# First modulation columns of a transformer block: whole rows, six of eight on VectorE and two on TensorE

## The reference, cut to what matters

```
mods = (silu(c) @ w_ada + b_ada).reshape(B, 9, 1024)     # c: 1024, w_ada: 1024 x 9216
n = rmsnorm(x, g_pre[0]) * (1 + scale(0)) + shift(0)     # shift(0), scale(0): first 2048 columns
f = (silu(n @ w_gate) * (n @ w_up)) @ w_down             # 1024 -> 2816 -> 1024
h = x + 0.5 * gate(0) * rmsnorm(f, g_post[0])
```

## Time and profile before

| | |
|---|---|
| median of three executions | 1119.7 us (1119.01 to 1119.9) |
| the profiled execution: time, span | 1119.9 us, 1118.2 us |
| TensorE products busy | 1077.9 us (96%) |
| TensorE weight loads busy | 939.3 us (84%) |
| VectorE busy | 853.0 us (76%) |
| ScalarE busy | 549.4 us (49%) |
| DMA | 266.65 MB, mean 238 GB/s |
| chain that ended last | TensorE 84%, VectorE 6%, DMA 3%, ScalarE 3% |
| mean granted clock of TensorE | 0.989 |

### The profile page before, as it was taken

One profiled execution on the slowest core, in us unless ns is written; L12 is line 12 of the kernel. 1 busy time (PEld: TensorE's weight loads), 2 busy tenths in 40 slices (PEclk: granted clock), 3 DMA queues, 4 the chain that ended last, 5 costly groups with the idle time before them and its releaser, 6 DMA issues.

```text
span 1118.2 us, 16397 instructions
## 1 busy us (share of the span) xinstructions
PE 1077.9 (96%) x6258; PEld 939.3 (84%) x6258; DVE 853.0 (76%) x914; ACT 549.4 (49%) x666; POOL 48.1 (4%) x78
## 2 busy tenths in 40 slices
PE   5799999999999999999999999999999999999996
PEld 3699999979988798888878888888888878888886
DVE  6888888668977787887868988877775787666664
ACT  4434434464675744444464454446454456444442
POOL 0000000011031100000010000001100000000001
PEclk9799999999999999999999999999999999999999
DMA  8899997636433589887569999744553546666641
GB/s 304 312 388 400 398 385 281 208 100 230 152 114 120 181 306 327 310 303 251 195 239 344 342 362 336 250 141 165 187 182 107 162 139 213 222 220 229 207 169 57
DMA packets 147045, 266.65 MB, mean 238 GB/s; under 512 B 9673, under 2 KB 104246, under 8 KB 141750
## 3 DMA queue, kind: packets, MB, share of 16 engines
q1 hardware_dynamic: 145104, 262.69, 67.4%
q0 software_dynamic: 1056, 3.17, 0.8%
q10 hardware_dynamic: 838, 0.15, 0.1%
HBM read 263.34 MB, written 2.65 MB: 238 GB/s over the span
## 4 chain that ended last, share of the span: by engine, by line
PE 84%; DVE 6%; DMA 3%; ACT 3%; issue 2%; POOL 1%; SPq 1%; POOLq 0%; ACTq 0%; DVEq 0%
PE ps L1861 16%; PE ps L1796 12%; PE ps L1798 11%; PE ps L1797 11%; PE ps L1863 8%; PE ps L1842 7%; PE ps L1845 7%; PE ps L1844 7%; DMA w_raw<-in_w_ffn_up 2%; DVE arena L1377 1%; DMA arena<-in_w_ada 1%; DVE w_lo L1150 1%; ACT w_hi L785 1%; ACT nT_both L785 1%; ACT nT L811 1%
## 5 line engine op out<-in xcount | busy, mean ns | idle before, releaser
L1150 DVE TENSOR_TENSOR w_lo<-w_raw,w_hi 128x2048 fp32r<-128x2048 f32 (+3 forms) x170 | 383.1, 2258 | 113.3 <-ACT w_hi L785 112.1
L785 ACT ACTIVATE w_hi<-w_raw 128x2048 fp32r<-128x2048 f32 (+3 forms) x170 | 320.0, 1886 | 272.4 <-PE ps L1798 115.5
L1861 PE MATMUL ps<-nT_both,w_hi 128*128 128x512 f32 x768 | 272.0, 398 | 0.0
L1863 PE MATMUL ps<-nT_both,w_lo 128*128 128x256 f32 x768 | 215.6, 281 | 0.0
L1842 PE MATMUL ps<-nT_both,w_hi 128*128 128x256 f32 x672 | 191.4, 285 | 0.3 <-DVE h_act L1261 0.2
L1845 PE MATMUL ps<-nT_both,w_lo 128*128 128x256 f32 x672 | 190.1, 283 | 0.0
L1844 PE MATMUL ps<-nT_both,w_hi 128*128 128x256 f32 x672 | 190.1, 283 | 0.0
L1861 PEld LDWEIGHTS ps<-nT_both,w_hi 128*128 128x128 f32 x768 | 144.3, 188 | 35.7
L1863 PEld LDWEIGHTS ps<-nT_both,w_lo 128*128 128x128 f32 x768 | 145.0, 189 | 0.9
L1842 PEld LDWEIGHTS ps<-nT_both,w_hi 128*128 128x128 f32 x672 | 128.8, 192 | 2.0 <-DVE h_act L1261 1.2
L1229 DVE SCALAR_TENSOR_TENSOR arena<-arena,c_act 128x3072 f32<-128x3072 f32 (+2 forms) x49 | 129.4, 2650 | 1.3 <-DMA arena<-in_ada_w 0.7
(11 more groups left out here) (278 smaller groups left out, 1203.8 us busy)
## 6 DMA issues: line engine op xcount, KB each, us to landing
arena<-in_w_ada SPq DMA_DIRECT2D x16, 1536.0 KB, 10.5
arena<-in_ada_w SPq DMA_DIRECT2D x16, 1536.0 KB, 8.7
w_raw<-in_w_in SPq DMA_DIRECT2D x46, 512.0 KB, 4.6
w_raw<-in_w_ffn_down SPq DMA_DIRECT2D x44, 512.0 KB, 4.5
w_raw<-in_ffn_w_down SPq DMA_DIRECT2D x44, 512.0 KB, 4.2
w_raw<-in_w_ffn_gate SPq DMA_DIRECT2D x42, 512.0 KB, 6.8
w_raw<-in_w_ffn_up SPq DMA_DIRECT2D x42, 512.0 KB, 8.7
w_raw<-in_ffn_w_gate SPq DMA_DIRECT2D x42, 512.0 KB, 4.1
```

What stands on the lines that cost most here:

```text
L785: copy = lambda o, i: act.activation(o, i, ACT.Copy)
L1150: dve.tensor_tensor(lo(s, n), raw(s, n), hi(s, n).bitcast(F32), ALU.subtract).then_inc(lo_ready[s], 1)
L1861: pe.matmul(ps[:, i, :], hi(s)[:, cols], nT_both[:, kk].rearrange("p a n -> p (a n)"), start=(kk == 0), stop=False, skip_group_check=True)
L1863: last = pe.matmul(ps[:, i, 0:S], lo(s)[:, cols], nT_hi[:, kk, :], start=False, stop=(kk == KD - 1), skip_group_check=True)
```

## The change

The eight pieces of four rows by 512 columns become sixteen rows: for each half eight rows j, each with the 512 columns of shift and the 512 of scale together (`[P, 2, 512]`, 512 KB, in the same runs of 2 KB). Rows 0 to 5 (`ON_DVE`) are summed by VectorE as one vector of 1024 columns (`first_rows`), with one fold of 1024 columns and one fold product for each half. Rows 6 and 7 (`ON_PE`) are not summed by VectorE: `first_rows_sum` on TensorE takes 128 columns of the row as weights and `c_act[:, 0, j]` as one moving column, 8 products for a row, 16 for a half, into a bank of their own. `first_folded` adds the bias to the folded part (four operations), `first_out` adds TensorE's part (one operation) and makes the scale columns. SyncE loads the first weights ahead of rows 6 and 7; it waits for VectorE's sums before it loads over a row, and for TensorE's sum before rows 6 and 7 of half 1; the fourth weights go out after rows 0 and 1 of half 1 are summed. On VectorE the low part of the first weights moves ahead of the last step of half 0's columns. On TensorE the fold products move a little, and `first_rows_sum` stands right before the first products (half 0), and behind the fold product (half 1).

```diff
--- before.py
+++ after.py
@@ -118,10 +118,10 @@
         last_gain = carve(4 * ADA, D)
         e_raw = carve(4 * ADA, PIECE)
         first_acc = carve(4608, 2, NB)
-        first_raw = carve(2 * ADA, 3, 2 * D)
-        first_at = [first_raw[:, 0], first_raw[:, 1], first_raw[:, 2], gate[:].rearrange("p a n -> p (a n)"),
-                    first_raw[:, 0], w_raw[:, SLOT_B], first_raw[:, 1], first_raw[:, 2]]
-        first_free = {4: 1, 6: 2, 7: 4}
+        first_raw = carve(2 * ADA, 6, D)
+        slots = [first_raw[:, i] for i in range(6)] + [gate[:, i, :] for i in range(2)] + \
+                [w_raw[:, SLOT_B, i * D:(i + 1) * D] for i in range(2)]
+        first_at = [slots[0:8], slots[8:10] + slots[0:6]]
         pick = carve(18688, P)
         folds = carve(18688 + P, 4, Q)
         gate_folds = vec_rows[:, 1, 2 * Q:4 * Q].rearrange("p (i q) -> p i q", q=Q)
@@ -187,7 +187,6 @@
         rel_ready = sem("rel_ready")
         first_sum, first_mods = map(sem, ["first_sum", "first_mods"])
         first_loaded = [sem(f"first_loaded{i}") for i in range(KD)]
-        last_part = sem("last_part")
         ada_loaded = [sem(f"ada_loaded{s}") for s in range(2)]
         ada_done = [sem(f"ada_done{s}") for s in range(2)]
         pick_ready = sem("pick_ready")
@@ -276,7 +275,7 @@
         }
-        FOLDS = ["shift 0", "scale 0", "shift 1", "scale 1", "F0", "F0 late", "F1", "F2", "F2 late", "F3"]
+        FOLDS = ["first 0", "rows 0", "first 1", "rows 1", "F0", "F0 late", "F1", "F2", "F2 late", "F3"]
         fold_cols = {
             "F0": [(D, 0, 3, 1), (2 * D, 0, 4, 1)],
             "F0 late": [(4 * D, 0, 6, 2), (5 * D, 0, 7, 2)],
@@ -310,7 +309,13 @@
         n_ada = {"F0": 0, "F1": 8, "F2": 16, "F3": 24}
-        FIRST = [(m, half, q) for half in range(2) for m in range(2) for q in range(2)]
+        ON_DVE, ON_PE = range(0, 6), range(6, KD)
+
+        def folded_to(group):
+
+            i = FOLDS.index(group) + 1
+            return (i + 1) // 2 if i <= 4 else i - 2
+
         gain_at = {1: (0, 80), 2: (0, 88), 3: (1, 72), 4: (1, 80), 5: (1, 88)}
         w_in = a["w_in"][0].rearrange("(k p) n -> p k n", p=P)
@@ -554,7 +559,8 @@
             def ffn_loads(f, next_e, next_b):
                 if f == "F0":
-                    sp.wait_ge(first_sum, KD)
+                    sp.wait_ge(first_sum, 2 * len(ON_DVE))
+                    sp.wait_ge(fold_mm, FOLDS.index("rows 1") + 1)
                 else:
                     load_gu(f, 0, 1)
                     load_gu(f, 1, 1)
@@ -593,32 +599,32 @@
             sp.dma_start(onehot[0:BUCKETS, :], a["onehot"]).then_inc(rel_loaded, 16)
             src = w1.rearrange("(p j) n -> p j n", j=KD)
-            def load_first(i):
-                if i in first_free:
-                    sp.wait_ge(first_sum, first_free[i])
-                m, half, q = FIRST[i]
-                c0 = m * D + half * NB
-                parts = 2 if i % 4 == 3 else 1
-                js = 4 // parts
-                for part in range(parts):
-                    j = js * part
-                    dst = first_at[i][:, j * NB:(j + js) * NB].rearrange("p (j n) -> p j n", n=NB)
-                    done = last_part if part else first_loaded[i]
-                    sp.dma_start(dst, src[:, 4 * q + j:4 * q + j + js, c0:c0 + NB]).then_inc(done, 16)
-
-            for i in range(2):
-                load_first(i)
+            def load_first(half, j):
+                dst = first_at[half][j].rearrange("p (m n) -> p m n", n=NB)
+                cols = src[:, j, 0:2 * D].rearrange("p (m n) -> p m n", n=D)[:, :, half * NB:(half + 1) * NB]
+                sp.dma_start(dst, cols).then_inc(first_loaded[j], 16)
+
+            for j in range(4):
+                load_first(0, j)
             for t in range(T):
                 sp.dma_start(x_res[:, t, :], a["x"][0, t * P:(t + 1) * P, :]).then_inc(x_loaded, 16)
-            for i in range(2, 4):
-                load_first(i)
+            for j in range(4, 6):
+                load_first(0, j)
             load_gu("F0", 0, 0)
-            load_first(4)
+            for j in ON_PE:
+                load_first(0, j)
+            sp.wait_ge(first_sum, 2)
+            for j in range(2):
+                load_first(1, j)
             load_gu("F0", 0, 1)
-            for i in range(5, KD):
-                load_first(i)
+            for j in range(2, 6):
+                sp.wait_ge(first_sum, j + 1)
+                load_first(1, j)
             load_gu("F0", 1, 0)
-            sp.wait_ge(first_sum, 6)
+            sp.wait_ge(fold_mm, FOLDS.index("rows 0") + 1)
+            for j in ON_PE:
+                load_first(1, j)
+            sp.wait_ge(first_sum, len(ON_DVE) + 2)
             load_gu("F0", 1, 1)
             sp.wait_ge(toe_sb, H)
@@ -1359,70 +1365,65 @@
             dve.tensor_copy(pick[:, Q:P].rearrange("p (r q) -> p r q", q=Q),
                             pick[:, 0:Q].rearrange("p (o q) -> p o q", o=1).broadcast_to([P, P // Q - 1, Q])).then_inc(pick_ready, 1)
             dve.wait_ge(c_ready, 1)
-            def first_piece(i):
-
-                m, _, q = FIRST[i]
-                acc = first_acc[:, m, :]
-                for j in range(4):
+            first_sums = first_acc.rearrange("p m n -> p (m n)")
+
+            def first_rows(half, js):
+
+                for j in js:
+                    dve.wait_ge(first_loaded[j], 16 * (half + 1))
+                    row, c = first_at[half][j], c_act[:, 0, j:j + 1]
                     if j == 0:
-                        dve.wait_ge(first_loaded[i], 16)
-                    if j == 2 and i % 4 == 3:
-                        dve.wait_ge(last_part, 16 * (i // 4 + 1))
-                    row, c = first_at[i][:, j * NB:(j + 1) * NB], c_act[:, 0, 4 * q + j:4 * q + j + 1]
-                    if q == 0 and j == 0:
-                        link(dve.tensor_scalar(acc, row, c, None, ALU.mult))
+                        dve.tensor_scalar(first_sums, row, c, None, ALU.mult).then_inc(first_sum, 1)
                         continue
-                    if j == 0:
-                        dve.wait_ge(first_sum, i)
-                    last = dve.scalar_tensor_tensor(acc, row, c, acc, ALU.mult, ALU.add)
-                    if j < 3:
-                        link(last)
-                last.then_inc(first_sum, 1)
-
-            def first_fold(m, half):
-
-                dve.wait_ge(first_sum, 4 * half + 2 * m + 2)
-                dve.tensor_reduce(folds[:, 2 * half + m, 0:16], first_acc[:, m, :].rearrange("p (r q) -> p r q", q=Q), AX.X, ALU.add,
+                    dve.wait_ge(first_sum, len(ON_DVE) * half + j)
+                    dve.scalar_tensor_tensor(first_sums, row, c, first_sums, ALU.mult, ALU.add).then_inc(first_sum, 1)
+
+            def first_fold(half):
+
+                dve.wait_ge(first_sum, len(ON_DVE) * (half + 1))
+                dve.tensor_reduce(folds[:, half, :], first_sums.rearrange("p (r q) -> p r q", q=Q), AX.X, ALU.add,
                                   apply_transpose=True).then_inc(folded, 1)
-            def first_out(m, half):
-
-                group = f"{('shift', 'scale')[m]} {half}"
+            def first_folded(half):
+
+                k = slice(4 * half, 4 * half + 4)
+                group = f"first {half}"
                 dve.wait_ge(fold_mm, FOLDS.index(group) + 1)
-                k = slice(4 * half, 4 * half + 4)
                 for g in range(P // Q):
                     rows = slice(g * Q, (g + 1) * Q)
-                    last = dve.tensor_tensor(mod_col[rows, 0, 1 - m, k], ps[rows, fold_bank(group), g:16:P // Q],
-                                             vec_col[rows, 0, KD * m + 4 * half:KD * m + 4 * half + 4], ALU.add)
+                    last = dve.tensor_tensor(mod_col[rows, 0, 1::-1, k],
+                                             ps[rows, fold_bank(group), g:Q:P // Q].rearrange("p (m k) -> p m k", k=4),
+                                             vec_col[rows, 0, 0:2 * KD].rearrange("p (m k) -> p m k", k=KD)[:, :, k], ALU.add)
                 link(last)
-                if m:
-                    dve.scalar_tensor_tensor(mod_col[:, 0, 0, k], mod_col[:, 0, 0, k], 1.0,
-                                             vec_col[:, 0, 72 + 4 * half:76 + 4 * half], ALU.add, ALU.mult).then_inc(first_mods, 1)
-
-            first_piece(0)
-            first_piece(1)
-            first_fold(0, 0)
-            first_piece(2)
-            first_piece(3)
-            first_fold(1, 0)
+
+            def first_out(half):
+
+                k = slice(4 * half, 4 * half + 4)
+                group = f"rows {half}"
+                dve.wait_ge(fold_mm, FOLDS.index(group) + 1)
+                link(dve.tensor_tensor(mod_col[:, 0, 1::-1, k], mod_col[:, 0, 1::-1, k],
+                                       ps[:, fold_bank(group), 0:KD].rearrange("p (m k) -> p m k", k=4), ALU.add))
+                dve.scalar_tensor_tensor(mod_col[:, 0, 0, k], mod_col[:, 0, 0, k], 1.0,
```

(53 more changed lines are left out.)

## The result

The changed kernel took **1122.64 us** in the median of 20 executions (1119.57 to 1125.6), the kernel before 1119.77 us (1118.04 to 1122.62, 20). The ratio is 1.0022, 95% interval 1.0013 to 1.003: slower by about 2.5 us (the medians differ by 2.9), where 0.9 us of gain were forecast. Its executions also spread more, over 6.0 us and not 4.6. Its profiled execution took 1120.59 us (span 1118.9), so it is one of the quick ones, and the first lesson is what one profile of such a kernel does not show.

A forecast was written before the change was run, and what follows sets the result against it. DMA bounds the opening, then TensorE; the gain is the earlier end of half 1's columns, moving later loads. Span 1118.2 − 0.9 = 1117.3, plus 1.7 around it, less 0.2 for the median: 1118.8 us, range 1116.5 to 1121.6.

The forecast's parts named there:

- M1: End of the last small operation making half 1's scale and shift columns: 47.90 us before, forecast 0.3 to 1.5 earlier.
- S0: Start of TensorE's first product of half 0: 29.67 us before, forecast 28.8.
- S1: Start of TensorE's first product of half 1: 50.59 us before.
- C2: Start of TensorE's chunk 2, at 70.69 us in the first profile of the kernel before.
- Landings, VectorE's part, the move of the low part: Opening: row 5 lands at 18.2 us, first weights' low part ends at 25.3, half 1's VectorE fold at 42.2.
- M0: End of the last small operation making half 0's scale and shift columns: 26.99 us before, forecast 26.6 to 27.4.
- I take 0.22: TensorE's row matmuls: 0.22 us per two-pass matmul at full clock, 3.5 us for the 16 of a half.
- rows at the half clock: Rival: half 0's 32 passes on TensorE take 0.23 us each, +2.7 us, 1122.4 us; chance 0.10.
- So the gain that arrives is the shift of M1, through the start of this DMA train: Loads from 50.20 us lead to TensorE's chunk at 88.06; only the shift of M1 arrives, taken as 0.9 us.
- Half-clock stretches: Rival: TensorE's stretch at 233.5 us is spared, 1.7 us, 1117.1, chance 0.17; or one comes elsewhere, 1120.5.
- Smaller loads: Rival: 512 KB row loads land later in the opening, at 4.2 us a MiB, giving 1124.6 us; chance 0.03.
- Nothing arrives: Rival: TensorE's late start and rows in half 1 use up VectorE's gain, 1119.7 to 1120.1; 0.18 with a new stretch.

The follow-up runs named there:

- the early load: First gate/up piece of chunk 2 loaded ahead of the table store: kernel before 1118.28 us (0.9989); changed kernel 1119.65 (0.9999), again 1118.43 (0.9995).
- extra products: Changed kernel plus five TensorE products nobody reads, around the transposes and rows of half 0: 1120.95 us (1.0005).
- rows 6 and 7 early: Changed kernel with rows 6 and 7 of half 1 loaded behind row 5, ahead of the third weights: 1120.79 us (1.0021).
- rows in the middle: Changed kernel with half 1's rows loaded early and taken by TensorE amid chunk 1's products, before channel block 1: 1122.4 us (1.0021).

## Why the prediction was wrong

Two steps failed. Rows that were taken to run at the full clock often don't, and the lead at M1 did not go through the DMA train to TensorE. Where the time went can be summed from profiles. Four of the changed kernel and two of the one before:

| profile (time) | rows of half 0, half 1 | S0 | S1 | C2 (idle before) | C2 to the end | half-clock stretches behind C2, without the one at the very end |
|---|---|---|---|---|---|---|
| before (1119.9) | | 29.67 | 50.59 | 70.69 (0.20) | 1047.5 | 1 |
| before, again (1119.15) | | 29.54 | 50.45 | 71.43 (2.00) | 1046.0 | 0 |
| changed (1120.59) | 3.98, 3.71 | 29.41 | 50.18 | 71.70 (2.49) | 1047.2 | 1 |
| changed, again (1123.44) | 4.45, 4.61 | 29.50 | 51.16 | 73.00 (2.08) | 1048.7 | 2 |
| changed, third (1122.79) | 5.71, 3.91 | 31.44 | 52.41 | 73.87 (2.63) | 1047.2 | 1 |
| changed, fourth (1124.44) | 6.94, 3.71 | 31.51 | 52.30 | 74.09 (2.11) | 1048.6 | 2 |

The changed kernel's mean span is 1121.1, that of before 1117.8: +3.3 us, a little above the measured +2.9 and +1.5. These are few executions, from more than one chip, so the shares below are rough. It splits into three. S1 is 1.0 later (51.5 for 50.5). From S1 to C2 it takes 21.6 and not 20.5, 1.1 more. And behind C2 stand 1.5 half-clock stretches and not 0.5, 1.2 more. In all profiles without the early load, that part without one lasts 1046.0 to 1046.2 in three profiles, with one 1047.1 to 1047.5, with two 1048.6 to 1048.7.

**Landings, VectorE's part, the move of the low part: right.** Row 5 began at 18.67 for 18.2, the low part of the first weights ended at 25.98 (25.3 forecast), VectorE's second fold at 43.02 (42.2). S0 came 1.9 behind M0 (1.8).

**"I take 0.22", the rows at the full clock: the first step that failed.** Both prices were near: 3.7 to 4.0 us and 6.94 to 6.96 for the 32 passes, for 3.5 and 7.4. The chance was not. I gave 0.10 to rows at the half clock, because in the one profile the clock read 1.00 from 22.0 to 25.2. Of nine profiles with this code and no extra products, one is 3.84, one 3.98, two about 4.5, and five lie from 5.71 to 6.96. The stretch at full clock that the rows need begins between 21.4 and 23.0, or isn't there. The sign was in the profile of before: the last argument against the rival was that the clock "stood at 1.00 until 25.2" while TensorE's transposes lay in front, but these transposes took (2.87 − 0.42) / 11 = 0.22 us a pass, the half-clock pace, and the recorded stretch lasted only from 21.9 to 25.3:

```profile
18.73 2.87 PE L1812 MATMUL ps<-ident,y_row 128*128 128x128 f32 x12
```

The kernel before had nothing on TensorE there that M0 waits for: 29.67 and 29.54 in its two profiles, where the changed kernel has 29.4 to 31.5. That term alone is up to 2 us at S0, or 3.5 where row 6 is late as well. It makes single executions slow. The loss in the median needs more: it is clear of noise only in versions with rows on TensorE in both halves and without extra products or the early load (1.0022 and 1.0011, rows 6 and 7 early 1.0021, rows in the middle 1.0021), and not with half 0, half 1 or both on VectorE (1.0006, 1.0002, 1.0003), though these intervals overlap. Even in the first profile only 0.4 of the 0.9 us forecast had arrived at M1 (47.50).

**"So the gain that arrives is the shift of M1, through the start of this DMA train": the second.** I let the train be a fixed length and the chunk at 88.06 its end. In the second profile of before and the first of the changed kernel the chain of waits has nothing but TensorE there; the gate is C2, and the train's length varies: 15.6 and 16.5 us to ScalarE in the two profiles of before, 17.0 to 17.3 in the four of the changed kernel. With M1 at 46.89, 1.0 earlier than before, C2 was 71.0, within the two values of before. Loading a piece ahead of the train took the wait away in all five profiles: −1.65 us by the medians for the kernel before, and from 1.0022 and 1.0011 to 0.9999 and 0.9995 for the changed one. So a gap between 50 and 72 is in both kernels, and closing it measured more (0.2 to 2.2 us by the interval) than the 0.9 that the change aimed at.

**Half-clock stretches: that they come and go was right, the price too high** (1.7 taken, 1.2 for the first and 1.4 for the second, by the means of the groups above), and I counted with one at a time. The changed kernel had one that began between 234 and 239 in all four profiles and in two another right behind the wait at C2.

**Smaller loads**: no cost that can be told (1.0003). **Nothing arrives** (1119.7 to 1120.1): the time of the best executions, not of the median.

What stays open: why the train is longest in profiles with rows on TensorE in both halves (16.9 to 17.3 us in five of seven, 16.7 in the two others; 15.6 to 16.8 in the versions with rows in one half or none). In the traces it is the last of 16 parts of a transfer that comes 0.5 to 1.0 us behind the fifteenth, against 0.1 to 0.3 in the two of before; I found no transfer that the change adds beside it. And what decides in an execution whether the clock rises at 22 is not known. That rows of half 0 at half pace go with long times rests on the four profiles of the changed kernel and on the pairs with and without extra products (spread 5.6 against 3.1 and 5.6 against 2.3; but 4.1 against 4.1 for the changed kernel itself); how much of the +2.9 in the median they make is only summed from profiles, and no experiment separates it.

## What to carry to other kernels

Work that waits behind a gate should not be put on an engine in a stretch where its clock is not settled: the price of 32 small matmuls was 3.8 to 7.0 us from one execution to the next, and TensorE's next products followed. A forecast that rests on the granted clock of a short stretch, or on a wait of 0.2 us, needs a second profile of the same kernel; one more profile of the kernel before would have shown a wait of 2.0 us at C2. When a lead vanishes behind a full transfer queue, look for a hole in the queue earlier on: moving one load into it was worth 1.65 us by the medians, with no other change.

## What the runs showed of the hardware that I had not expected

- A two-pass product with 128 columns of weights and one moving column costs about what 64 moving columns cost (0.22 us for two passes): 0.12 us a pass at 2.4 GHz (3.71 for 32), 0.22 at 1.2 GHz (6.95 for 32).
- The same code at the same place finds the full clock in some executions and not in others, and the profile's clock reads 1.00 where no record exists (the fourth profile of the changed kernel, before 36.8).
- Idle time of 2 to 3 us on TensorE in front of C2 was followed by a half-clock stretch of 3.4 us in three profiles (73.3, 74.3, 74.8) and by none in four others (2.00, 2.26, 2.49 and 2.63 us idle).
- The train of transfers took 15.6 and 16.5 us in two profiles of one kernel, and up to 17.3 in the changed one. The last of 16 parts came 0.1 to 1.0 us behind the fifteenth, which is a part of the difference.
